# SSD steps of a hybrid backbone: z projected one step later, chunks 0 and 1 mixed ahead of the taps of B, a rewritten drain

## What is computed

```
z, xbc, dt = split(h @ w_in)
xbc = silu(dwconv_centred(xbc, conv_w, conv_b))      # 5 taps; gives xs, B, C
cum = cumsum(dt * a);  seg = cum[l] - cum[s]
scores = (C B^T) * exp(masked seg)
y  = scores @ (xs * dt) + (C * exp(cum)) @ h         # intra-chunk and inter-chunk parts
h' = h * exp(cum_end) + B^T (tail * xs * dt)         # state
out = rms_norm(y * silu(z)) @ w_out
```

## Time and profile before

| | |
|---|---|
| median of 3 runs | 1758.17 us (1756.37 to 1759.17) |
| profiled execution, its own time | 1754.64 us |
| its span, first to last instruction | 1753.4 us |
| mean granted TensorE clock | 0.912 of 2.4 GHz |
| PE / DVE / ACT / POOL busy | 1565.6 / 1120.2 / 733.8 / 303.9 us |
| layer 0, steps 0 to 8 | about 113 to 583 us of the span |
| layer 3, steps 0 to 8 | about 1377 to 1707 us |

### The profile page before, as it was taken

One profiled execution on the slowest core, in us unless ns is written; L12 is line 12 of the kernel. 1 busy time (PEld: TensorE's weight loads), 2 busy tenths in 40 slices (PEclk: granted clock), 3 DMA queues, 4 the chain that ended last, 5 costly groups with the idle time before them and its releaser, 6 DMA issues.

```text
span 1753.4 us, 22888 instructions
## 1 busy us (share of the span) xinstructions
PE 1565.6 (89%) x8633; PEld 1283.8 (73%) x8633; DVE 1120.2 (64%) x1694; ACT 733.8 (42%) x1291; POOL 303.9 (17%) x379
## 2 busy tenths in 40 slices
PE   5699999999976999988878999989999899998877
PEld 2577877777765789766556877767788788887766
DVE  0257888887777465655645645535336778888875
ACT  1435444544434334355453522322334445554442
POOL 0011433343333101100000000000001023322330
PEclk7589999999978999999989989989899899999888
DMA  9432455335440322222432143442441343343333
GB/s 287 136 91 81 121 144 160 112 113 151 139 144 24 108 96 79 82 73 73 144 121 84 49 147 111 151 144 73 144 138 38 88 130 99 100 116 97 99 106 108
DMA packets 169422, 197.40 MB, mean 113 GB/s; under 512 B 9696, under 2 KB 151648, under 8 KB 169312
## 3 DMA queue, kind: packets, MB, share of 16 engines
q1 hardware_dynamic: 158480, 163.08, 29.2%
q0 software_dynamic: 9296, 30.19, 6.8%
q10 hardware_dynamic: 1536, 2.67, 0.5%
HBM read 194.59 MB, written 1.31 MB: 112 GB/s over the span
## 4 chain that ended last, share of the span: by engine, by line
PE 53%; DVE 28%; ACT 8%; issue 8%; DMA 2%; ACTq 0%; POOL 0%; DVEq 0%
PE ps L400 14%; PE ps L401 13%; PE ps L402 13%; DVE xc L809 6%; DVE w_lo L369 4%; PE ps L424 3%; DVE cum_b L817 3%; PE ps L562 2%; PE ps L568 2%; DMA raw<-in_mod_w 2%; ACT Wb L714 2%; DVE Wb L836 2%; DVE Hs L851 1%; ACT w_hi L362 1%; PE ps L1624 1%
## 5 line engine op out<-in xcount | busy, mean ns | idle before, releaser
L400 PE MATMUL ps<-h_hi,w_hi 128*128 128x512 f32 (+1 forms) x1056 | 407.1, 386 | 14.5 <-DVE w_lo L369 14.0
L401 PE MATMUL ps<-h_lo,w_hi 128*128 128x512 f32 (+1 forms) x1056 | 393.7, 373 | 0.0
L402 PE MATMUL ps<-h_hi,w_lo 128*128 128x512 f32 (+1 forms) x1056 | 393.2, 372 | 0.0
L369 DVE TENSOR_TENSOR w_lo<-raw,w_hi 128x1024 fp32r<-128x1024 f32 (+1 forms) x205 | 244.4, 1226 | 148.9 <-ACT w_hi L362 147.3
L362 ACT ACTIVATE w_hi<-raw 128x1024 fp32r<-128x1024 f32 (+1 forms) x205 | 208.1, 1049 | 135.8 <-PE ps L402 126.6
L400 PEld LDWEIGHTS ps<-h_hi,w_hi 128*128 128x128 f32 x1056 | 202.9, 192 | 60.9 <-issue 26.1
L402 PEld LDWEIGHTS ps<-h_hi,w_lo 128*128 128x128 f32 x1056 | 202.3, 192 | 34.9
L401 PEld LDWEIGHTS ps<-h_lo,w_hi 128*128 128x128 f32 x1056 | 202.9, 192 | 32.5
L809 DVE SCALAR_TENSOR_TENSOR xc<-ps,gp,xc 128x508 f32<-128x508 f32 (+1 forms) x224 | 162.7, 728 | 41.8 <-ACT xc L683 35.8
L400 PE MATMUL ps<-w_hi,h_hi 128*128 128x512 f32 (+2 forms) x368 | 134.3, 365 | 21.1 <-DVE w_lo L369 18.4
L402 PE MATMUL ps<-w_hi,ylo 128*128 128x512 f32 x384 | 151.5, 395 | 0.0
(11 more groups left out here) (236 smaller groups left out, 2795.2 us busy)
## 6 DMA issues: line engine op xcount, KB each, us to landing
raw<-in_mod_w SPq DMA_DIRECT2D x96, 512.0 KB, 4.7
raw<-in_ssm_w_in SPq DMA_DIRECT2D x64, 512.0 KB, 5.1
cum_b<-cum_scratch POOLq DMA_DIRECT2D x96, 256.0 KB, 5.0
raw<-in_ssm_w_in SPq DMA_DIRECT2D x66, 256.0 KB, 3.9
raw<-in_ssm_w_out SPq DMA_DIRECT2D x32, 512.0 KB, 4.6
raw<-in_pool_w_in SPq DMA_DIRECT2D x32, 512.0 KB, 4.6
raw<-in_attn_w_in SPq DMA_DIRECT2D x20, 512.0 KB, 3.9
raw<-in_pool_w_out SPq DMA_DIRECT2D x16, 512.0 KB, 4.4
```

What stands on the lines that cost most here:

```text
L369: dve.tensor_tensor(lo[:, 0:width], raw[:, r % RS, 0:width], hi[:, 0:width].bitcast(F32), ALU.subtract).then_inc(lo_done, 1)
L400: pe.matmul(o, hi_s, hi_m, start=first, stop=False)
L401: pe.matmul(o, hi_s, lo_m, start=False, stop=False)
L402: return pe.matmul(o, lo_s, hi_m, start=False, stop=last)
```

## The change

Step 0 now projects only x, B and C. In steps 1 to 7 the slots k = 4 and 5 take z of the group before, and step 8 takes z of group 7, so its place in the drain is the same. Weight pieces are loaded and split in the new order: z of group g where z of group i was, z of group 7 at the end of step 7. `mix` is divided into `weigh_steps` (L836) and `mix` (L839). The weighings of chunks 0 and 1 stand right after the split of z, the mixes of 0 and 1 before `taps(2)`. In layer 3 the same names mean chunks 2 and 3. POOL does `forward_part` 2 and 3 ahead of `pool_squares`. The drain has a list of its own on ACT and DVE, and on PE `stage_a` 0 and 1 stand behind `pe_scan_ctx` (in layer 3 `stage_a` 1 stands behind `pe_scan_lat`).

```diff
@@ items
                 add_piece("w", L, "bc", i)
-                add_piece("w", L, "z", i)
+                if i:
+                    add_piece("w", L, "z", i - 1)
...
+            add_piece("w", L, "z", GRP - 1)
@@ ssd_pe_step
-            if i < GRP - 1:
+            if has_ssd:
                 ssd_project(pe, L, i, 4)
...
-            if i < GRP - 1:
+            if has_ssd:
                 ssd_project(pe, L, i, 5)
...
-        ssd_project(pe, L, GRP - 1, 4)
+        ssd_project(pe, L, GRP, 4)
         pe_turn_inputs(pe, L, g)
-        ssd_project(pe, L, GRP - 1, 5)
+        ssd_project(pe, L, GRP, 5)
         pe_turn_y(pe, L, g - 1)
         pe_states(pe, L, g, 0)
         pe_states(pe, L, g, 1)
-        stage_a(pe, L, 0)
         pe_states(pe, L, g, 2)
         if not last_layer(L):
             pe_scan_ctx(pe, L, g)
-        stage_a(pe, L, 1)
+        stage_a(pe, L, 0)
+        if not last_layer(L):
+            stage_a(pe, L, 1)
         pe_scan_lat(pe, L, g)
+        if last_layer(L):
+            stage_a(pe, L, 1)
         pe_turn_y(pe, L, g)
@@ ssd_act_step
         if not has_in:
-            z_silu(GRP - 1, 0)
+            z_silu(g, 0)
+            turned()
+            cb_dt(0)
+            cb_dt(1)
+            z_silu(g, 1)
+            exps((0, 1))
+            for c in range(4):
+                act_yhi(act, L, c)
+            for c in (2, 3):
+                act_split(act, L, "out", c, 0)
+            squares(g - 1)
+            exps(range(2, nc))
+            for n in range(2, nc):
+                cb_dt(n)
+            for c in range(4, 12):
+                act_yhi(act, L, c)
+            squares(g)
+            return
...
-            act_split2(act, L, "z", i)
+        if has_ssd:
+            act_split2(act, L, "z", g)
...
+            act_split2(act, L, "z", i)
             for c in (0, 1):
                 act_split(act, L, "out", c, 0)
@@ ssd_dve_step
+        if not has_in:
+            y_lat(i - 2)
+            decay(0)
+            decay(1)
+            masks()
+            gate(i - 2)
+            weigh_steps(0)
+            weigh_steps(1)
+            state(0)
+            state(1)
+            mix(0)
+            mix(1)
+            state(2)
+            for c in range(4):
+                dve_ylo(dve, L, c)
+            for c in (2, 3):
+                dve_split(dve, L, "out", c, 0)
+            for n in range(2, nc):
+                decay(n)
+            if not last_layer(L):
+                y_ctx(g)
+            for n in range(2, nc):
+                weigh_steps(n)
+                mix(n)
+            y_lat(g)
+            gate(g)
+            return
...
         if has_ssd:
+            dve_split2(dve, L, "z", g)
+            weigh_steps(0)
+            weigh_steps(1)
             decay(1)
             state(0)
             state(1)
             for n in range(2, nc):
                 decay(n)
-        if has_in:
-            taps(2)
+            mix(0)
+            mix(1)
+        taps(2)
         if has_ssd:
             state(2)
-            mix(0)
-            mix(1)
@@ ssd_pool_step
+        for n in range(2, nc):
+            forward_part(n)
         if g:
             pool_squares(pool, L, g - 1)
-        for n in range(2, nc):
-            forward_part(n)
```

More of the change, by code:

```diff
@@ L508, in ssd_project @@
             t0 = SEG
-        project(pe, proj_bank(i, k), (L, what, i), k % 2, s[what + "_p"], t0)
+        project(pe, proj_bank(i, k), (L, what, i if k < 4 else i - 1), k % 2, s[what + "_p"], t0)
     def pe_turn_inputs(pe, L, g):
@@ L716, in cb_dt, with exps @@
             last.then_inc(s["cbdt_a"], 1)
-        def exps():
-            for n in range(nc):
+        def exps(ns):
+            for n in ns:
                 act.wait_ge(s["seg_d"], 2 * nc * g + 2 * n + 2)
@@ L738, in ssd_act_step @@
             turned()
-        if has_in:
-            first_tap(0)
+        first_tap(0)
         if has_ssd:
@@ L743, in ssd_act_step @@
             cb_dt(1)
-        if has_in:
-            first_tap(1)
-            silu(0)
-            act_split2(act, L, "z", i)
[L748 to L755, removed]
+        first_tap(1)
+        silu(0)
+        if has_ssd:
+            act_split2(act, L, "z", g)
+        silu(1)
+        first_tap(2)
         if i >= 2:
@@ L758, in ssd_act_step @@
         if has_ssd:
-            exps()
+            exps(range(nc))
         if mods:
             act_mod_rows(act, L + 1, q, 6)
[L762 to L766, removed]
+        first_tap(3)
+        silu(2)
         if has_ssd:
+            z_silu(g, 0)
             for n in range(2, nc):
                 cb_dt(n)
[L770 to L776, removed]
+        silu(3)
+        if i + 1 < GRP:
+            act_split2(act, L, "x", i + 1)
+        else:
+            act_split2(act, L, "z", i)
+            for c in (0, 1):
+                act_split(act, L, "out", c, 0)
         if mods:
             act_mod_rows(act, L + 1, q + 1, 6)
[L779 to L784, removed]
+        if has_ssd:
+            z_silu(g, 1)
     def ssd_dve_step(dve, L, i, T):
@@ L830, in masks, with weigh_steps @@
                                   ALU.mult).then_inc(s["cbm_d"], 1)
-        def mix(n):
-            c = first + n
+        def weigh_steps(n):
             dve.wait_ge(s["cbdt_a"], nc * g + n + 1)
@@ L836, in mix @@
             T["w_d"].inc(dve.tensor_tensor(Wb[:, n % 2, :, :], Wb[:, n % 2, :, :], Wa[:, n % 2, :, :], ALU.add))
-            T["w_d"].wait(dve)
+        def mix(n):
+            c = first + n
+            dve.wait_ge(s["w_d"], nc * g + n + 1)
             dve.wait_ge(s["exp_a"], nc * g + n + 1)
@@ L893, in ssd_dve_step @@
             decay(0)
-        if has_in:
-            taps(0)
+        taps(0)
         if has_ssd:
@@ L899, in ssd_dve_step @@
             gate(i - 2)
[L900 to L907, removed]
+        taps(1)
         if has_ssd:
+            dve_split2(dve, L, "z", g)
+            weigh_steps(0)
+            weigh_steps(1)
             decay(1)
@@ L913, in ssd_dve_step @@
                 decay(n)
[L914 to L915 removed]
+            mix(0)
+            mix(1)
+        taps(2)
         if has_ssd:
             state(2)
[L918 to L919 removed]
         if mods:
             dve_mod_col(dve, L + 1, q, 6, 256)
[L922 to L923 removed]
+        taps(3)
         if has_ssd:
             for n in range(2, nc):
+                weigh_steps(n)
                 mix(n)
[L927 to L930, removed]
[L931 to L932 removed]
+        if i + 1 < GRP:
+            dve_split2(dve, L, "x", i + 1)
+        else:
+            dve_split2(dve, L, "z", i)
+            for c in (0, 1):
+                dve_split(dve, L, "out", c, 0)
         if has_ssd and not last_layer(L):
@@ L936, in ssd_dve_step @@
             dve_mod_col(dve, L + 1, q + 1, 6, 256)
-        if i == GRP:
-            y_lat(g)
-            gate(g)
     def ssd_pool_cum(pool, L, g, cs):
```

20 lines of the change are left out of this document (11 added, 9 removed).

## The result

| | before | changed |
|---|---|---|
| median of 16 runs | 1759.16 us (1756.12 to 1761.29) | 1762.43 us (1759.41 to 1768.01) |
| profiled execution, own time / span | 1754.64 / 1753.4 us | 1765.47 / 1764.2 us |
| mean granted clock | 0.912 | 0.927 |

The ratio is 1.0022, 95% interval [1.0012, 1.0031]: slower by 0.22%, 2.1 to 5.5 us. The forecast was slower, by 8.8 us, with a range of 1747 to 1781 us. The direction and the place of the loss came out. The size is well under half of the forecast: DVE's loop did not grow, and the steps of layer 3 did not get longer by what was put down for them.

The account below looks back on a forecast made before the run. PE with its hole bounds layer 0's steps, DVE's loop close behind. Terms -4 + 5.4 + 5.7 - 8.3 + 5.5 + 4.5 = +8.8 us on 1754.6 give 1763.4, or 1767 on the median; range 1747 to 1781 us.

Parts of the forecast that it names:

- The hole closes: Layer 0, steps 3 to 6: PE's 1.66 and 1.00 us waits for mixes 0 and 1 vanish, nothing to spare.
- The price of 2.6 us: Layer 0, steps 3 to 6: average lengthening of DVE's loop by the low clock at the latent scan.
- It even grows ... +0.8 us. Loop: 53.1 us: Layer 0, steps 3 to 6: a fourth POOL-DVE blocking lengthens DVE's loop by 0.8, bounds 0 and +1.6.
- About every second step: +0.8 each, six steps, +4.9: Layer 3, steps: later latent scan; low clock lasting into project 0 costs 1.6 us in about every second step.
- Start of layer 0: Layer 0, steps 0 to 2: less PE work in step 0, hole closed in step 1; -4, bounds -6 and -1.
- Drain of layer 0: Layer 0, drain: PE waits fall from 11.8 to 7.5 us, shorter low clock; -8.3, bounds -12 and -4.
- Step 7: Layer 0, step 7: split of z of group 7, loop growth and low clock make 58.1 us, +5.7.
- Drain of layer 3: Layer 3, drain: later ylo and splits, possible late DMA of cum_b; +4.5, bounds 0 and +7.
- High clock: Rival: the clock stays high at layer 0's latent scan, steps 2 to 7; -13, 1745 us; chance 0.25.
- Even: Rival: low clock falls in PE's spare time, layer 0 steps 54.8 us, layer 3 hides its scan; 1758; chance 0.15.
- The hole stays: Rival: squares and exps wait for POOL's forward_part, so PE still waits for the mix; 1775 us; chance 0.08.
- slower still: Rival: late DMA in layer 3's drain, low spell into project 0 nearly every step, both layers; 1777 us; chance 0.15.

Follow-up runs that it names:

- the matmul run: Changed kernel with 12 matmuls of 512 columns before PE's wait for the second mod_col, layer 0 steps 2 to 7: 1746.3 us, 0.9931.
- the old drain of layer 3: Changed kernel with the drain of layer 3 alone back in its old order on PE, ACT and DVE: 1753.49 us, 0.9980.
- state 2: Changed kernel with DVE's state(2) ahead of taps(2) instead of behind it: 1767.64 us, 1.0047.
- the early x of step 0: Changed kernel with the next x split ahead of the taps of B and C in step 0 of layers 0 and 3: 1750.31 us, 0.9952.
- The two experiments on the kernel before: Kernel before with the second mod_col ahead of y_ctx: 1756.62 us, 0.9990; kernel before with sixteen matmuls in the context scan's two waits: 1755.55 us, 0.9984.
- the combined version: Changed kernel with state(2), mod_col and next x moved earlier, layer 3's old drain, output weight splits 0 and 1 last in step 7: 1723.78 us, 0.9798.
- the mod_col run: Changed kernel with the second mod_col ahead of y_ctx on DVE, steps 2 to 7 of layer 0: 1743.1 us, 0.9912.
- four in 0.9 us: Four matmuls in the second mod_col wait, layer 0 steps 2 to 7, on the combined version with layer 3's next x ahead of taps(3): 1698.93 us, 0.9668.

## Where the prediction held, and which of its steps failed

**Layer 0, steps 3 to 6: the term that was mis-sized.** "The hole closes", the waits of 1.4 and 3.1 us (0.94 and 3.1 measured), the low clock over the latent scan and its place on DVE's loop all hold. The price of 2.6 us is about right: 2.7 where the scan ran low, 1.7 in the one step in four where the clock fell later, 2.5 on average. The step that failed is "It even grows ... +0.8 us. Loop: 53.1 us". The loop is 52.24 (the matmul run), which is the 52.3 read off the trace before with nothing added. The added blocking was reasoned from the order of POOL's list, and four meetings for three did occur, but together they cost 2.6 us for 2.5. Four steps of 0.86 us are 3.4 of the 3.9 us missed in this stretch; the bound of 0 that was written beside it was the value. The steps were 53.9 to 55.1 us, mostly under the 55 to 56 named as the sign of being right. It is not one lucky execution: the runs with the old drain of layer 3, with state 2 and with the early x of step 0 have the same DVE work in these steps, and their averages are 54.7, 54.7 and 55.2 us for the 55.7 forecast.

**Layer 3, steps: the second term that failed.** "About every second step: +0.8 each, six steps, +4.9" was too much. The scan waits 2.55 us (2.8 forecast), and the low spell stays hidden in four steps of six, which take 37.87; two take 39.52. So the price of such a step, 1.6 us, was right, and two had it, not three. What failed more is the base that it was added to. The steps of the kernel before are 37.8, 37.8, 38.2, 38.5, 39.1 and 37.8, which I took as 37.8 each. Over 37.8 a step the six are 3.7 us after and 2.5 before, hence +1.2. Even that is within what one execution differs from the next. The two experiments on the kernel before leave its layer 3 as it was, and with it their steps 2 to 7 take 229.3, 229.1 and 231.7 us; in the changed kernel and the runs with the twelve matmuls, the old drain and `mod_col` they take 230.5, 228.9, 230.5 and 228.8. No cost of the change can be read there.

**Terms that held.** Start of layer 0: -6.1 for -4, with PE standing still 12.6 us as forecast. Drain of layer 0: -7.1 to the turn of y against -8.3 (waits of 3.8 and 2.8 for 3.5 and 2.5), -6.0 to the output product.

**Step 7: right in part by luck.** +5.7 forecast, +6.0 measured. The split of z on DVE is there. But 0.8 us of the sum was loop growth that did not come, and the wait of 3.7 us for `mod_rows`, which ACT makes behind the output splits, was not in it. In the run with the twelve matmuls step 7 still takes 57.2 us, with 3.5 us of this wait, where DVE's loop and the split would be 52.24 + 2.36 = 54.6. With the output splits moved behind `mod_rows`, in the combined version, the wait is gone.

**Drain of layer 3.** +7.3 for +4.5. The two causes named are there (`ylo` late by 4.7 us, the last DMA of `cum_b` issued 4.64 us late, as before). How far they were priced too low is open, because the drain of before is not one number: it took 47.4 us in the trace of the kernel before, and 51.8 and 51.7 in the two experiments on that kernel, whose drain is the same. In these two DVE's L819 takes 4.08 and 4.00 us instead of 0.69, beside a group of POOL (run with `mod_col` on the kernel before):

```profile
1671.66 4.08 DVE L819 TENSOR_TENSOR cum_b<-cum_b 128x512 f32<-128x512 f32 x1
1671.72 3.47 POOL L968 TENSOR_TENSOR xw<-xT,sg 128x256 f32<-128x256 f32 x6
```

In the trace of the kernel before, L819 began 0.63 us ahead of POOL's group and took 0.69. Against 51.7 the new drain (54.5 and 54.8 in three profiles) costs 3 us, and the touched stretches come to +1.2 us instead of +5.5; the +3.3 of the medians lies between. How often each case comes in the runs without a profile is not known.

Together, in this pair of traces: -3.9 and -3.7 on the steps and -2.1 at the start of layer 0, against +2.8 and +2.3 in the drains, +1.0 at the start of layer 3 and +0.3 in step 7. That is 3.3 us under the forecast of 8.8 and gives the 5.5 us of the touched stretches.

**The rivals.** High clock would have needed a clock of 1.00 at the scan: it was 0.59, and the run that forced 1.00 was 0.9% faster than the changed kernel (1746.3 us, where the rival had 1745), so that rival had its price about right and its condition wrong. The Trainium skill (TensorE: Matmul & The Clock Gate, HAM oscillation) names long gaps as what drops the clock; here the rows show it dropping behind waits of 3.1 us, of 1.22 us and of 0.93 us, with short matmuls of 64 columns behind them, and the measurement decides: no long gap was needed. "Even" came nearest to the measured size, and its steps of 54.8 us to the measured 54.7, though not by its reason: the low clock is not in PE's spare time, it costs 2.5 us a step on a loop of 52.24. "The hole stays" is out, since no wait for the mix is left in steps 2 to 6. Of "slower still" the late DMA came, the low spell in nearly every step of layer 3 did not.

## What to carry to other kernels

When a hole on the fullest engine is closed, first write down the next engine's loop (here S to S, 52.3 us against PE's 48.5) and what a wait inside it will do to the clock; the gain ends there, and a cheap reorder inside the new loop (`mod_col` ahead of `y_ctx`, 1.1%) may be worth more than the change itself. Test such a reorder on the kernel before and after: that it is worth nothing before and much after says which engine is the bound. An idle share is not a gain: taking one wait of 2.55 us away gave another of 3.79.

## What was not expected of the hardware

With the same instructions and the same two waits of 0.93 us in every step, the clock fell behind the scan in steps 4 and 5 of the mod_col run and not in 3 and 6 (51.7 and 50.0 us, above). In layer 3 of the run with the twelve matmuls the sixteen intra matmuls take 2.13, 2.44, 2.73 and 3.02 us in four following steps of 37.9 us, 0.3 us more each time, though the wait before them is 2.56 us in all four. The fall depends on more than the wait right before it, and equal steps need not have equal clocks.

Matmuls that compute nothing needed, in a wait that exists anyway, cost no time that shows and gave 0.9% (twelve in 3.1 us) and, by one profile each, some 5 us (four in 0.9 us). In the kernel before, sixteen in two waits gave 0.2% only, because the clock fell behind the next wait.

Two orders of POOL's list gave the same total of blocking on DVE, 2.5 and 2.6 us a step. But one instruction can lose far more than that: the 0.69 us of L819 became 4.08 in the drain of layer 3, and in the two traces that show such a blocking the drain is 4 us longer.
